# Early transposes of the prompt's queries and keys, compression inside retention, and attention units ordered head by head

## The reference, cut to what matters

```
h  = rmsnorm(x) @ w_in                      # (512, 3872), all branches side by side
q  = heads(h.nsa_q)                         # 8 heads of 64; kv: 6 x 2 heads of 64
rows = [k_cmp, v_cmp, rope(k_sel), v_sel];  win = [rope(k_win), v_win]
k_c, v_c = compress(k_cmp), compress(v_cmp) # 31 blocks: 2 matmuls, SiLU, 1 matmul
o_cmp = softmax(q . k_c, causal by block) v_c
o_sel = softmax(rope(q) . k_sel, causal) v_sel   # 512 positions have 8 blocks, all are selected
o_win = softmax(rope(q) . k_win, causal) v_win   # the window of 512 covers the prompt
no = (g0*o_cmp + g1*o_sel + g2*o_win) * silu(h.nsa_g)
y  = x + rmsnorm([retention, no, delta] @ w_out)
```

## Time and profile before

| | |
|---|---|
| median of 3 runs | 2633.17 us (2610.85 to 2634.86) |
| profiled execution | 2642.13 us |
| its span | 2640.5 us |
| TensorE busy | 2229.7 us, 84% of the span |
| VectorE busy | 1321.1 us, 50% |
| ScalarE busy | 730.7 us, 28% |
| DMA | 242.04 MB, mean 92 GB/s |
| mean granted clock of TensorE | 0.854 of full speed |

### The profile page before, as it was taken

One profiled execution on the slowest core, in us unless ns is written; L12 is line 12 of the kernel. 1 busy time (PEld: TensorE's weight loads), 2 busy tenths in 40 slices (PEclk: granted clock), 3 DMA queues, 4 the chain that ended last, 5 costly groups with the idle time before them and its releaser, 6 DMA issues. The chain is left out here.

```text
span 2640.5 us, 35927 instructions
## 1 busy us (share of the span) xinstructions
PE 2229.7 (84%) x12280; PEld 1657.8 (63%) x12280; DVE 1321.1 (50%) x3088; ACT 730.7 (28%) x1512; POOL 302.4 (11%) x516
## 2 busy tenths in 40 slices
PE   6989748738999999997889896586499999999977
PEld 3644448737767888886354444486376678888863
DVE  1252566534654666654213434765355556666532
ACT  2120002103434454440212101111044445444302
POOL 0000000000013433420000000000000234334100
PEclk9999769756879999996989997687567889999859
DMA  4443010020027886851035330100300368868420
GB/s 148 147 151 113 26 35 1 1 79 7 1 52 168 192 188 152 181 124 72 2 113 168 137 109 10 35 1 2 84 1 1 89 150 191 179 152 190 107 72 36
DMA packets 175947, 242.04 MB, mean 92 GB/s; under 512 B 50118, under 2 KB 132838, under 8 KB 175084
## 3 DMA queue, kind: packets, MB, share of 16 engines
q1 hardware_dynamic: 151180, 172.51, 24.5%
q0 software_dynamic: 24576, 67.14, 10.8%
HBM read 223.17 MB, written 24.97 MB: 94 GB/s over the span
## 5 line engine op out<-in xcount | busy, mean ns | idle before, releaser
L601 PE MATMUL bank<-W,hT 128*128 128x512 f32 (+3 forms) x1152 | 449.0, 544 | 30.6 <-DMA W<-in_w_in 21.5
L1282 POOL DMA_DIRECT2D SHARED<-in_cache_nsa_kv x256 | 151.5, 592 | 2048.7 <-issue 734.4
L601 PEld LDWEIGHTS bank<-W,hT 128*128 128x128 f32 x1152 | 219.0, 195 | 230.8 <-issue 184.5
L1225 PE MATMUL bank<-XT,W 128*128 128x256 f32 (+1 forms) x768 | 250.8, 462 | 0.0
L1214 ACT ACTIVATE XT<-bank 128x512 f32<-128x512 f32 x256 | 140.3, 593 | 132.6 <-PE bank L1207 132.5
L1282 POOL DMA_DIRECT2D PS<-in_cache_nsa_kv x256 | 150.7, 589 | 140.6 <-issue 128.2
L1225 PEld LDWEIGHTS bank<-XT,W 128*128 128x128 f32 x768 | 134.9, 190 | 49.7 <-issue 36.9
L1207 PE MATMUL bank<-CF,RP 128*128 128x128 f32 x1024 | 146.9, 290 | 7.6 <-DVE RP L1195 6.9
L1708 PE MATMUL bank<-QBD,PS 128*128 128x64 f32 x1024 | 141.9, 287 | 0.0
L1501 DVE TENSOR_REDUCE mx<-bank 128x1 f32<-128x31 f32 (+4 forms) x192 | 74.6, 389 | 132.5 <-PE bank L1443 131.1
L1708 PEld LDWEIGHTS bank<-QBD,PS 128*128 128x128 f32 x1024 | 139.7, 210 | 0.7
(11 more groups left out here) (378 smaller groups left out, 3699.4 us busy)
## 6 DMA issues: line engine op xcount, KB each, us to landing
SHARED<-in_cache_nsa_kv SPq DMA_DIRECT2D x256, 128.0 KB, 6.1
SHARED<-in_cache_nsa_kv POOLq DMA_DIRECT2D x256, 128.0 KB, 5.3
PS<-in_cache_nsa_kv SPq DMA_DIRECT2D x256, 128.0 KB, 6.1
PS<-in_cache_nsa_kv POOLq DMA_DIRECT2D x256, 128.0 KB, 5.7
W<-in_w_in SPq DMA_DIRECT2D x48, 512.0 KB, 4.5
XS<-scratch_conv_p SPq DMA_DIRECT2D x24, 384.0 KB
PW<-in_state_nsa_win SPq DMA_DIRECT2D x16, 512.0 KB, 3.8
Wo<-in_w_out SPq DMA_DIRECT2D x4, 2048.0 KB, 11.8
```

Of the source, the lines that this page charges most:

```text
L601: return nc.tensor.matmul(bk((c * NTILE + t) % 8)[:, 0:b - a], hT[:, k, t * P:(t + 1) * P], W[:, k // 2, k % 2, 0:b - a], start=(k == 0), ...
L1225: mm = nc_(self.v).tensor.matmul(out, self.v['W1'][:, kv, s, :], seg[:, s], start=(s == 0), stop=(s == SEG // PAIRS - 1))
L1282: e.dma_start(where[side * HD:(side + 1) * HD, slot, :, :], A['cache_nsa_kv'][l, page].rearrange("(p r) a g d -> p r (a g d)", r=PAIRS)[:, ...
```

## The change

Four things are changed.

First, x is stored to memory at the start of `project` (into `scratch_q_rot`, which the queries no longer use, and `out_y_sample`) and read back in `out_project`. In between, the tile `X` holds `QT` and `KT`.

Second, the 40 transposes of queries and keys move into chunks 7 and 8 of the projection (`key_turn`, `query_turn`), through PSUM bank 7, which the products give up (`BANKS` is 7); ScalarE copies them out. Rotated queries stay in `MIX` and `QR`, and neither the stores nor the load of queries remain.

Third, the compression moves into `retention`, beside steps that the table `BESIDE` names, and so do the loads of its weights. The first block of `prompt_attention` is gone.

Fourth, attention's units run head by head through the branches 1, 2, 0; each branch has its own output bank (4, 5, 7), so the score ring has three banks. `KT` and `KC` hold both key heads in 128 rows without zeros, and `scores` takes the 64 rows of the head's group (`o:o + HD`) of keys and queries.

```diff
 project
-    NC, RING = len(chunks), 4
+    NC, RING, BANKS, TURNS = len(chunks), 4, 7, 7
+            e.dma_start(A['q_rot'].rearrange("(t p) d -> p t d", p=P), X[:, 0:4, :]).then_inc(kept, 16)
+            e.dma_start(O['y_sample'].rearrange("b t d -> (b t) d"), X[0:64, 4, :]).then_inc(kept, 16)
...
-                dve.wait(e, f"nqc{j}")
-                e.dma_start(A['q_rot'][j * P:(j + 1) * P, :], QR[:, :, :].rearrange("p i c -> p (i c)")).then_inc(rot, 16)
...
-            for c in range(6, NC):
-                copies(e, c, 0)
+            copies(e, 6, 0)
+            e.wait_ge(kept, 32)
+            for t in range(4):
+                pe.wait(e, f"tk{t}")
+                act.done(e, f"tk{t}", nc.scalar.activation(KT[:, :, t * P:(t + 1) * P], bk(TURNS, 4)[:, 0:2, :], ACT.Copy))
+            copies(e, 7, 0)
+            for t in range(4):
+                for i in range(2):
+                    pe.wait(e, f"tq{t}{i}")
+                    act.done(e, f"tq{t}{i}", nc.scalar.activation(QT[:, i, :, t * P:(t + 1) * P], bk(TURNS, 4), ACT.Copy))
+            copies(e, 8, 0)
...
-                        if j == 0 and u >= 8:
-                            e.wait_ge(e_dve if u % 2 else e_act, (u - 8) // 2 + 1)
+                        if j == 0 and u >= BANKS:
+                            e.wait_ge(e_dve if (u - BANKS) % 2 else e_act, (u - BANKS) // 2 + 1)
...
+                        if c == 7 and j == 1 and t < 4:
+                            key_turn(t)
+                        if c == 8 and j < 2 and t < 4:
+                            query_turn(2 * j + t // 2, t % 2)
 retention
+    BESIDE = {("norm", 0): ["R0", "R1"], ("back", 1): ["T0", "T1", "X0", "X1"], ("back", 3): ["H0", "HT0"], ("norm", 3): ["A0", "HS0"],
+              ("back", 4): ["C0", "H1", "C0k", "HT1", "A1", "HS1"], ("norm", 4): ["C1", "C1k"]}
 prompt_attention
-    DEEP = 4
-    sbank = lambda u: bk((0, 1, 6, 7)[u % DEEP])
+    DEEP = 3
+    BRANCHES = (1, 2, 0)
+    OUT = {1: 4, 2: 5, 0: 7}
+    sbank = lambda u: bk((0, 1, 6)[u % DEEP])
-    units = [(qt, br, h) for qt in range(4) for br in range(3) for h in range(NH)]
+    units = [(qt, br, h) for qt in range(4) for h in range(NH) for br in BRANCHES]
...
-                kt = KCG[:, g, 0:n] if br == 0 else KT[:, g, br - 1, 0:n]
-                nc.tensor.matmul(sbank(u)[:, 0:n], QT[:, min(br, 1), r, qt * P:(qt + 1) * P], kt, start=True, stop=False)
+                o = g * HD
+                kt = KC[o:o + HD, 0:n] if br == 0 else KT[o:o + HD, br - 1, 0:n]
+                nc.tensor.matmul(sbank(u)[:, 0:n], QT[o:o + HD, min(br, 1), r, qt * P:(qt + 1) * P], kt, start=True, stop=False)
...
-                if h == 0 and q >= 2:
-                    e.wait_ge(merged, q - 1)
+                if h == 0 and qt:
+                    e.wait_ge(merged, 3 * (qt - 1) + BRANCHES.index(br) + 1)
...
-                if u >= 3 and (u - 3) % NH == NH - 1:
+                if u >= 3 and units[u - 3][2] == NH - 1:
                     merge(u - 3)
 out_project
+            e.dma_start(X[:, 0:4, :], A['q_rot'].rearrange("(t p) d -> p t d", p=P)).then_inc(back, 16)
+            e.dma_start(X[0:64, 4, :], O['y_sample'].rearrange("b t d -> (b t) d")).then_inc(back, 16)
...
+            e.wait_ge(back, 32)
```

More of the change, by code:

```diff
@@ L678, in retention @@
             dn += [f"ss{k}{j}" for k in range(4) for j in "ms"] if t == 4 else []
-    with stage(["dve_s", "act_s", "pe_s", "loaded", "gl", "outs"]) as (block, (dve_s, act_s, pe_s, loaded, gl, outs)):
+            an += [f"sq{t}"]
+        beside = BESIDE.get((what, i), [])
+        pn += [f"{x}.p" for x in beside if x in ("T0", "T1", "H0", "C0", "H1", "C1")]
+        an += [f"{x}.p" for x in beside if x in ("X0", "X1", "HT0", "HS0", "HT1", "HS1")]
+        dn += [{"C0k": "C0.p", "C1k": "C1.p"}.get(x, f"{x}.p") for x in beside if x in ("R0", "R1", "A0", "C0k", "A1", "C1k")]
+    with stage(["dve_s", "act_s", "pe_s", "loaded", "gl", "rows", "small", "outs"]) as \
+            (block, (dve_s, act_s, pe_s, loaded, gl, rows, small, outs)):
         dve = Steps(dve_s, dn)
-        act = Steps(act_s, [f"sq{t}" for t in TILES])
+        act = Steps(act_s, an)
         pe = Steps(pe_s, pn)
@@ L686, in _ @@
             e.dma_start(gn[:, :], A['ret_gn'][l].partition_broadcast(P)).then_inc(gl, 16)
+            for i in range(2):
+                e.dma_start(PG[:, i, :, :], O['kv_prompt'][l, 0].rearrange("(t p r) a g d -> t p r (a g d)", p=P, r=PAIRS)[i, :, :, 0:256]).then_inc(rows, 16)
+            dve.wait(e, "z3")
+            for kv in range(2):
+                for half in range(2):
+                    for r in range(PAIRS):
+                        e.dma_start(W1[r * HD:(r + 1) * HD, kv, :, half * HD:(half + 1) * HD],
+                                    A['cmp_w1'][l, kv].rearrange("(h s r) d e -> h r d s e", h=2, r=PAIRS)[half, r]).then_inc(small, 16)
+                for g in range(G):
+                    e.dma_start(W2[:, kv, g, g * HD:(g + 1) * HD], A['cmp_w2'][l, kv]).then_inc(small, 16)
+            e.dma_start(v['B1'][:, :], A['cmp_b1'][l].rearrange("k e -> e k"), allow_slow_non_contiguous=True).then_inc(small, 16)
             dve.wait(e, "z2")
@@ L710, in _ @@
                 QK, ATT, KDc = QK_[:, i % 2], ATT_[:, i % 2], KDc_[:, i % 2]
+                if what == "norm":
+                    beside(what, i)
                 if what == "front":
@@ L755, in _ @@
                 pe.done(e, f"su{t}", mm)
+                beside(what, i)
         @block.vector
         def _(e):
+            dve.link(e, "z3", nc.vector.memset(W2[:, :, :, :], 0.0))
+            dve.done(e, "z4", nc.vector.memset(HS[:, :, :], 0.0))
             dve.link(e, "z1", nc.vector.memset(S[:, :, :], 0.0))
@@ L763, in _, with beside @@
             h3 = lambda ap: ap.rearrange("p (h c) -> p h c", c=HD)
+            def beside(what, i):
+                for x in BESIDE.get((what, i), []):
+                    if x in ("R0", "R1"):
+                        e.wait_ge(rows, 32)
+                        cp.side_by_side(e, dve, pe, int(x[1]), int(x[1]))
+                    if x in ("A0", "A1"):
+                        cp.join(e, dve, act, pe, int(x[1]))
+                    if x in ("C0k", "C1k"):
+                        cp.keep(e, dve, pe, int(x[1]))
             for what, i, t in ORDER:
@@ L2065, in out_project @@
     gpost = sb(scope, "gpost", [P, D])
[L2066 removed]
+    with stage(["w_left", "w_right", "gain", "back", "act_s", "dve_s", "pe_s"]) as \
+            (block, (w_left, w_right, gain, back, act_s, dve_s, pe_s)):
         pe = Steps(pe_s, [f"T{t}" for t in range(NTILE)] + [f"y{h}{t}" for h in range(2) for t in range(4)] + ["y04", "y14"])
```

247 lines of the change are left out of this document (104 added, 143 removed).

## The result

The changed kernel takes 2762.73 us (median of 4 runs, 2752.13 to 2771.85), the kernel before 2633.75 us in the same comparison. The ratio is 1.049, with a 95% interval of 1.044 to 1.054. The forecast was 2755 us. Every later kernel was timed beside the kernel before again, whose median then was 2625 to 2631 us.

A forecast was written before the change was run, and what follows sets the result against it. Attention is bound by TensorE at whichever clock is granted. Per layer -39.4 + 6 + 7 - 0.5 + 89 = +62 us, +124 in all, so 2755 us; this case spans 2713 to 2785, the overall range 2620 to 2795.

The forecast's parts named there:

- The stage that goes: Compress-and-transpose stage before attention: all of it goes with its barrier, -39.4 us a layer.
- Retention: Compression moved into retention: second set of products and VectorE's added work lengthen it, +7 us a layer, bounds 3.7 and 12.
- The projection: Chunks 7 and 8: early transposes 4.5 us and one PSUM bank fewer 1.8, together +6 us a layer.
- The delta rule's stage: Stage before attention in the changed kernel: it loses a memset, -0.5 us a layer.
- The clock: TensorE in attention: all of the new stage runs at 1.2 GHz; attention 255 us against 166.1, chance 0.68.
- attention's upper bound of +101: Upper end of attention's added time a layer, forecast +89 with bounds +67 and +101.
- the fall in the earlier trace: Kernel before, at 554.9: clock fell from 1.00 to 0.50 while 64-row passes ran, taken as evidence against 64 rows.
- Going in and out of 64 rows: Attention's switches of row count: 0.3 us a big unit, 0.1 a small one, 22 us a layer, bounds nothing to 31.
- Merges and ends: Attention: three merges at consecutive units stall 1.5 us, filling and draining take 7; together 8.5 us.
- rival 2: Attention at the upper clock throughout: 149 us, -44 us a layer, total 2545 us; chance 0.14.
- Rival 1: Attention: 64 rows do as well as 128, but the mixture keeps the clock down early; 188 us, total 2623; chance 0.15.
- Rival 3: Projection: copies or banks delay the early transposes, up to 20 us more a layer, 2795 us; chance 0.03.

The follow-up runs named there:

- late zeros: Changed kernel (64-row scores) plus sixteen 128-row products of zeros before the second head of the last query tile; 2724.59 us.
- early zeros: Changed kernel (64-row scores) plus sixteen 128-row products of zeros ahead of attention's first score; 2793.89 us.

## Why the prediction was right, and where it was not

**The stage that goes, and its parts elsewhere.** Forecast -39.4 + 6 + 7 - 0.5 = -26.9 us a layer, measured -26.8 in the mean of the layers. Retention was sized too high, +4.0 for +7, near the bound of 3.7 that takes only the second set of products; over the layers of all fourteen traces, 22 with the change and 6 without, it is 74.8 for 69.6, so +5.2. The projection was sized a little low: over the same layers it takes 289.3 us in the mean with the early transposes and 281.3 without, so +8. The delta rule's stage with the removed one came to -38.1 for -39.9, so it takes 1.3 us longer where half a microsecond less was forecast; the two layers of the kernel before differ there by 3.3 us. That the sum comes out so close is luck, since these errors cancel.

**The clock.** Forecast at 0.50 through the whole stage; that is what the profile shows, and changing the rows alone puts it there or takes it away, in both kernels. The price from the units at 1.2 GHz in the earlier trace rows held, because a stage without gaps has few other terms; that the whole stage is right to the microsecond is partly luck, as worked out below. One slip stands in the range: with attention's upper bound of +101 the sum is 2781 us and not 2785, which changes nothing here.

**Two of its reasons were wrong.** "Every third unit is a 31-key one, so no stretch of it looks like those in which the clock rose" carried half the argument. The order alone does not hold the clock down; if anything it makes the kernel faster, 2619.54 for 2626.52 us by itself and 2562.54 for 2581.94 with the rest of the change and 128 rows. And I read the fall in the earlier trace rows as the work of 64-row products. The late zeros show 64-row units that hold 2.4 GHz for 40 us. In the earlier trace rows the engine was busy in 2.72 of 3.30 us before the fall and in only 1.94 of 3.30 after it; those rows can't tell rows from gaps, and I should have said so. Only the narrow 64-row units do what I read there: behind the early zeros they lost 1.00 within 4.7 us with TensorE busy. What 64 rows do to wide units is to keep the clock from rising; since the stage starts at 0.50, that comes to the same.

**Going in and out of 64 rows.** Forecast 0.3 for a big unit and 0.1 for a small one. The 128-key units at 1.2 GHz, first with 64 rows, then in the new order with 128:

```profile
606.32 0.53 PE L1474 MATMUL bank<-UP,PT 128*128 128x64 f32 x2
606.77 0.79 PE L1451 MATMUL bank<-X 64*128 64x128 f32 x2
607.50 0.29 PE L1453 MATMUL bank<-CB 128*128 128x128 bf16 x1
```

```profile
626.50 0.53 PE L1467 MATMUL bank<-UP,PT 128*128 128x64 f32 x2
626.82 0.74 PE L1444 MATMUL bank<-KT,QT 128*128 128x128 f32 x2
627.36 0.31 PE L1446 MATMUL bank<-CB 128*128 128x128 bf16 x1
```

From the product with the values to the score it is 0.45 us for 0.32, and from the score to its mask 0.73 for 0.54. Together that is 0.32 for a big unit; small ones take 1.62 for 1.45. A head takes 6.70 in the second tile, where one with 128 rows at 1.2 GHz in the new order takes 5.98, and 10.97 in the last for the 10.31 priced: 0.72 and 0.66, where 0.7 was forecast. The weight loads of the same two scores:

```profile
606.77 0.50 PEld L1451 LDWEIGHTS bank<-X 64*128 64x128 f32 x2
```

```profile
626.72 0.55 PEld L1444 LDWEIGHTS bank<-KT,QT 128*128 128x128 f32 x2
```

With 128 rows the load begins 0.10 us ahead of its product (626.82), with 64 it begins together with it (606.77). The Trainium skill, TensorE: Matmul & The Clock Gate, section "Step-by-step: what each phase is for", says that weight loads are pulled ahead of running matmuls where the row groups don't conflict or the load goes to a background buffer; where the number of rows changes to 64, this trace does not show it.

**Merges and ends.** Forecast 1.5 us of stalls in all and 7 for both ends. The units show no stall: at the last boundary they go 3.61, 3.18, 2.04, 4.04, 3.61. The three merges are bare at the end instead:

```profile
835.14 0.17 DVE L1520 TENSOR_SCALAR fac<-SUM 128x8 f32<-128x8 f32 x1 [0.91 <-PE bank L1474]
...
841.23 0.69 DVE L1530 TENSOR_TENSOR MIX<-NO,UP 128x512 f32<-128x512 f32 x1
```

From the last score at 830.13 to the next stage are 13.1 us. From the first score to the last are 241.4 us, where the units were priced at 247, since the first of them run ahead of the full pipeline and the last one's transposes and values fall behind its score; the end, 13.1, is longer than the 8.5 forecast for stalls and ends. The two errors, -5.6 and +4.6, cancel to 254.5. At 2.4 GHz, as rival 2 priced them, there are stalls: with 128 rows in layer 1 the second head of the last tile takes 8.37 us for the later ones' 5.37.

**The rivals.** Rival 1, the mixture holding the clock down early, would be the kernel with the new order alone, and it isn't so: its first two tiles take 67 us, not the 89 worked out (78 without the switching of rows, which this kernel does not have). Rival 2, the upper clock throughout, gave 2545; the version that comes nearest, with 128 rows and lighter merges, reaches 2553 but still starts 39 us at 0.50 in layer 1. Rival 3 is excluded by the projection's +8.

## What to carry to other kernels

A product over 64 rows of the array is no shorter than one over 128 (a score of 512 columns took 2.07 us for 2.08 at 1.2 GHz, and 1.12 for 1.12 at 2.4), and where it stands in most units, as here, it can leave a gapless TensorE at half its clock: zero rows that fill the array may be worth more than the space and the memset that they cost. Read the granted clock beside the busy share before counting removed work, and cross the two halves of a bundled change; here the rows alone cost 166 us in the kernel before and 200 in the changed one, while all the rest of the change gains 64. A full engine is not yet a fast one.

## What the runs showed of the hardware that was not expected

- TensorE busy in 241.38 of 241.38 us at 1.2 GHz: a gapless stream did not raise the clock. It is not a matter of rows alone: narrow units with 128 rows stood at 0.50 with 38.58 us busy in 38.60, and in the other layer of the same kernel left it after 4.3 us.
- The clock has a memory. The same wide 64-row units ran at 0.50 for as long as they came in at 0.50, and at 1.00 for 40 us after 16.8 us of 128-row zeros. Why the narrow ones lost it within 4.7 us is open: rows, width and the filling of the pipeline weren't separated there; with 128 rows, narrow units between merges sat at 0.50 too (720 to 755 in the kernel with the widest tile first).
- Work added on purpose paid for itself twice: 26 us less with zeros beside every big unit, 38 us less with sixteen products in one place.
